# Summing both scan directions on chip, and starting the even layer's output product in the gate stage

## The reference, cut to what matters

```python
def head_group_norm(y, w, b):
    mean = jnp.mean(y, axis=-1, keepdims=True)
    var = jnp.mean(jnp.square(y - mean), axis=-1, keepdims=True)
    yn = (y - mean) * lax.rsqrt(var + RWKV_GN_EPS)
    return yn * w.reshape(RWKV_HEADS, RWKV_HEAD) + b.reshape(RWKV_HEADS, RWKV_HEAD)

def even_output(p, y, bon, conv_w, lnx_w, lnx_b, w_out):
    a_out = short_conv_branch(p[..., :A_COLS], conv_w)
    z_b = p[..., A_COLS + RWKV_SHIFT_COLS:]
    rw = head_group_norm(y, lnx_w, lnx_b) + bon
    b_out = rw.reshape(rw.shape[:2] + (RWKV_WIDTH,)) * jax.nn.silu(z_b.astype(jnp.float32))
    return jnp.concatenate([a_out, b_out.astype(p.dtype)], axis=-1) @ w_out
...
x = x + gate[:, None] * y_lat
```

## Time and profile before

| | us |
|---|---|
| median of 3 runs | 3437.85 (3435.22 to 3439.31) |
| the profiled execution's own time | 3434.52 |
| its span, first to last instruction | 3432.7 |
| TensorE busy | 3095.4 (90% of the span) |
| VectorE busy | 2020.2 (59%) |
| ScalarE busy | 1421.9 (41%) |
| GpSimd busy | 435.1 (13%) |

### The profile page before, as it was taken

How to read it: one execution, slowest core, us unless ns; L and a number is a source line. 1 busy time by engine, 2 the same in 40 slices (tenths; PEclk the granted TensorE clock), 3 DMA queues, 4 the chain that set the end, 5 groups by cost and what they waited for, 6 DMA issues and landing times. The chain is left out here.

```text
span 3432.7 us, 59566 instructions
## 1 busy us (share of the span) xinstructions
PE 3095.4 (90%) x25098; PEld 2564.0 (75%) x25098; DVE 2020.2 (59%) x2919; ACT 1421.9 (41%) x2147; POOL 435.1 (13%) x313
## 2 busy tenths in 40 slices
PE   8999998788874999797999999999667899999999
PEld 5878886777772879665999987777445778888887
DVE  6846345567665423353555534755343588888887
ACT  4434433333333223364444432443454455454443
POOL 0222221111111212200000012211011100000000
PEclk9999999799886999998999999999789999999999
DMA  8432223333314311325112113122111322222853
GB/s 306 131 129 106 97 86 125 76 77 85 78 43 166 127 57 62 125 91 175 54 56 62 39 61 128 50 61 90 62 41 45 115 84 78 90 77 78 301 165 123
DMA packets 216552, 343.65 MB, mean 100 GB/s; under 512 B 74208, under 2 KB 148064, under 8 KB 212832
## 3 DMA queue, kind: packets, MB, share of 16 engines
q1 hardware_dynamic: 192384, 252.43, 22.5%
q0 software_dynamic: 23040, 87.04, 7.4%
q10 hardware_dynamic: 864, 0.38, 0.0%
HBM read 243.72 MB, written 96.08 MB: 99 GB/s over the span
## 5 line engine op out<-in xcount | busy, mean ns | idle before, releaser
L60 PE MATMUL ev_ps<-h_hi,even_ring_hi 128*128 128x512 f32 (+1 forms) x792 | 288.0, 364 | 1.3 <-DVE late_area L806 1.3
L62 PE MATMUL ev_ps<-h_hi,even_ring_lo 128*128 128x512 f32 (+1 forms) x792 | 280.4, 354 | 0.0
L61 PE MATMUL ev_ps<-h_lo,even_ring_hi 128*128 128x512 f32 (+1 forms) x792 | 280.4, 354 | 0.0
L60 PE MATMUL ff_ps<-ff_op,ff_w_hi 128*128 128x512 f32 x672 | 263.6, 392 | 13.6 <-DVE ff_w_lo L3505 10.7
L62 PE MATMUL ff_ps<-ff_op,ff_w_lo 128*128 128x512 f32 x672 | 262.8, 391 | 0.0
L61 PE MATMUL ff_ps<-ff_op,ff_w_hi 128*128 128x512 f32 x672 | 262.7, 391 | 0.0
L60 PEld LDWEIGHTS ev_ps<-h_hi,even_ring_hi 128*128 128x128 f32 x792 | 149.6, 189 | 39.9 <-issue 19.8
L3072 ACT ACTIVATE ma_e<-ma_s,ma_nm 128x1280 f32<-128x1280 f32 x64 | 84.9, 1327 | 214.3 <-DVE ma_nm L3108 214.3
L61 PEld LDWEIGHTS ev_ps<-h_lo,even_ring_hi 128*128 128x128 f32 x792 | 149.7, 189 | 21.7 <-issue 1.7
L62 PEld LDWEIGHTS ev_ps<-h_hi,even_ring_lo 128*128 128x128 f32 x792 | 149.6, 189 | 21.2
L60 PEld LDWEIGHTS ff_ps<-ff_op,ff_w_hi 128*128 128x128 f32 x672 | 127.1, 189 | 41.0 <-DVE ff_w_lo L3505 14.5
(11 more groups left out here) (561 smaller groups left out, 8275.9 us busy)
## 6 DMA issues: line engine op xcount, KB each, us to landing
w_up_raw<-in_w_up SPq DMA_DIRECT2D x48, 512.0 KB, 4.4
w_up_raw<-in_w_down SPq DMA_DIRECT2D x34, 512.0 KB, 5.1
even_ring_raw<-in_ev_w_in POOLq DMA_DIRECT2D x33, 512.0 KB, 3.8
late_area<-in_ada_w SPq DMA_DIRECT2D x32, 512.0 KB, 5.3
ffn_mid<-h POOLq DMA_DIRECT2D x24, 512.0 KB, 2.9
ff_mem<-ffn_mid SPq DMA_DIRECT2D x24, 512.0 KB, 11.1
ar<-late_area SPq DMA_DIRECT2D x8, 1280.0 KB, 5.2
bk<-late_area SPq DMA_DIRECT2D x8, 1280.0 KB, 7.0
```

Of the source, the lines that this page charges most:

```text
L60: nc.tensor.matmul(out, w_hi, x_hi, start=start, stop=False, skip_group_check=resumed)
L61: nc.tensor.matmul(out, w_hi, x_lo, start=False, stop=False, skip_group_check=resumed)
L62: return nc.tensor.matmul(out, w_lo, x_hi, start=False, stop=stop, skip_group_check=resumed)
```

## The change

The y of both directions no longer goes to HBM. In the scan, GpSimd puts each half block into a resident array `ysum` (the tensor `y_even`, now in SBUF): the direction that reaches a token first copies, the other adds. `y` then holds only one half block for each d and e, and ScalarE's copy of the next block waits for GpSimd's sum of the one before. GpSimd also loads the first tile of the `odd_ring`, and makes its low part at the stage's end, where ScalarE makes its high part. The tiles of `ev_w_out` in the ring are laid out anew: a ring tile now holds one half (the convolution's or the scan's 512 input columns) of two output tiles m, so tiles 0 to 3 are the convolution's half and 4 to 7 the scan's.

The gate stage also multiplies the convolution's half. Its 24 units (m, token group) are each 4 steps of three matmuls into one of 5 PSUM banks; the first five units are taken side by side, step by step, as the parts of the convolution arrive. VectorE adds gate times each unit to x, which is loaded once, for all 8 tiles, and stays in SBUF. The mean and the variance share one PSUM area, so they alternate. The convolution's loads move from GpSimd's queue to SP's. The output stage then multiplies only the scan's half, 4 steps instead of 8 for each unit, and adds to the resident x.

```diff
-                def store(n):
-                    for d in range(2):
-                        at = first_token(d, n)
-                        done(sp, "y", d, n)
-                        sp.dma_start(g.yT[d][:, :, at:at + P], y[:, n % 2, d]).then_inc(yst[d, n % 2], 16)
-
                 load(0)
                 load(1)
-                for n in range(NB + 1):
-                    if n >= 1:
-                        store(n - 1)
-                    if n + 2 < NB:
-                        load(n + 2)
-                for d in range(2):
-                    for b in range(2):
-                        sp.wait_ge(yst[d, b], 16 * (NB // 2))
+                for n in range(2, NB):
+                    load(n)
...
+                load_tile(pool, ring, 0)
                 pool.wait_ge(consts, 96)
-                for n in range(NB):
+
+                def sum_outputs(n):
+                    if n + 1 < NB:
+                        for d in range(2):
+                            done(pool, "blocks", d, n + 1)
+                    for e in range(2):
+                        for d in range(2):
+                            at = first_token(d, n) + CH * ORDER[d][e]
+                            done(pool, "y", d, n, e)
+                            if comes_first(d, n):
+                                nc.gpsimd.tensor_copy(ysum[:, :, at:at + CH], y[:, d, e]).then_inc(S["ysum", d], 1)
+                            else:
+                                nc.gpsimd.tensor_tensor(ysum[:, :, at:at + CH], ysum[:, :, at:at + CH], y[:, d, e], ALU.add).then_inc(S["ysum", d], 1)
...
+                        if n >= 2:
+                            done(pool, "ysum", d, n - 2)
...
+                for n in range(NB + 1):
+                    if n < NB:
+                        masked_blocks(n)
+                    if n >= 1:
+                        sum_outputs(n - 1)
+                low_of_tile(nc, pool, ring, 0)
+                load_tile(pool, ring, 1)
...
-                        cp(y[:, n % 2, d, :, half(ORDER[d][e])], bC[d][:, 0:256].rearrange("c (p t) -> c p t", p=4)).then_inc(S["y1", d], 1)
+                        if n:
+                            done(act, "ysum", d, n - 1, e)
+                        cp(y[:, d, e], bC[d][:, 0:256].rearrange("c (p t) -> c p t", p=4)).then_inc(S["y1", d], 1)
...
+                high_of_tile(nc, act, ring, 0)
...
-def phase_even_gate(g, mix, ring):
+def phase_even_gate(g, conv_mix, mix, y, x, gate, ring):
...
+    UNITS = [(m, o, n) for m in range(KD) for o, n in GROUPS]
+    FREE = 5
...
+                def load_conv(p):
+                    if p >= 2:
+                        sp.wait_ge(conv_lo, p - 1)
+                    sp.dma_start(conv[:, p % 2], g.mixT[p]).then_inc(conv_in[p % 2], 16)
+
+                def load_x(m):
+                    sp.dma_start(x[:, m, 0:CTX], g.ins["ctxT"][:, m]).then_inc(x_in[m], 16)
+                    sp.dma_start(x[:, m, CTX:T], g.ins["xT"][:, m]).then_inc(x_in[m], 16)
+
+                load_conv(0)
+                load_conv(1)
+                load_x(0)
+                load_conv(2)
+                load_conv(3)
+                for m in range(1, KD):
+                    load_x(m)
...
+                load_extra(0)
+                load_extra(1)
+                for a in range(1, HALF + 1):
+                    low_of_tile(nc, pool, ring, a)
+                    load_tile(pool, ring, a + 1)
+                    if a + 1 < 4:
+                        load_extra(a + 1)
...
+                def step(u, k, resumed=False):
+                    m, o, n = UNITS[u]
+                    t, r = (m // 2) % 2, HALF * (m % 2) + k
+                    mm = product(nc, ps[:, u % FREE, 0:n], (ring.hi[:, t, r], ring.lo[:, t, r]), (c_hi[:, k, o:o + n], c_lo[:, k, o:o + n]),
+                                 k == 0, k == HALF - 1, resumed)
+                    if k == HALF - 1:
+                        mm.then_inc(done, 1)
+
                 mean_of(0)
-                for p in range(4):
-                    if p < 3:
-                        mean_of(p + 1)
-                    variance_of(p)
+                pe.wait_ge(ring.lo_done, 1)
+                for k in range(HALF):
+                    pe.wait_ge(conv_lo, k + 1)
+                    for u in range(FREE):
+                        step(u, k, resumed=True)
+                    if k == 1:
+                        variance_of(0)
+                for u in range(FREE, len(UNITS)):
+                    if u in (6, 10, 14):
+                        mean_of((u - 2) // 4)
+                    if u in (8, 12, 16):
+                        variance_of((u - 4) // 4)
+                    if u % (2 * NG) == 0:
+                        pe.wait_ge(ring.lo_done, u // (2 * NG) + 1)
+                    pe.wait_ge(added, u - FREE + 1)
+                    for k in range(HALF):
+                        step(u, k)
...
+                def split_tile(a):
+                    if a >= 2:
+                        act.wait_ge(done, 2 * NG * (a - 1))
+                    high_of_tile(nc, act, ring, a)
...
+                split_conv(0)
+                split_conv(1)
+                square(0)
+                split_conv(2)
+                split_conv(3)
+                scale(0)
+                split_tile(1)
+                for p in range(1, 4):
                     square(p)
...
+                    scale(p)
+                    split_y(p - 1)
+                    split_tile(p + 1)
                 split_y(3)
...
+                def add(first, last):
+                    for u in range(first, last):
+                        m, o, n = UNITS[u]
+                        if o == 0:
+                            dve.wait_ge(x_in[m], 32)
+                        dve.wait_ge(done, u + 1)
+                        stt(out=x[:, m, o:o + n], in0=ps[:, u % FREE, 0:n], scalar=gate(1 if o < CTX else 0)[:, m:m + 1], in1=x[:, m, o:o + n],
+                            op0=ALU.mult, op1=ALU.add).then_inc(added, 1)
...
                 centre(0)
-                add(2)
-                split_conv(0)
-                centre(1)
-                add(3)
-                split_conv(1)
-                gate(0)
-                centre(2)
-                split_conv(2)
-                gate(1)
-                centre(3)
-                split_conv(3)
-                split_y(0)
-                gate(2)
-                split_y(1)
-                gate(3)
-                split_y(2)
+                for p in range(4):
+                    split_conv(p)
+                gate_y(0)
+                add(0, 6)
+                for p in range(1, 4):
+                    u = 4 * p + 2
+                    centre(p)
+                    split_y(p - 1)
+                    add(u, u + 3)
+                    gate_y(p)
+                    add(u + 3, u + 4)
+                add(18, 20)
                 split_y(3)
+                add(20, 24)
...
-def phase_even_out(g, mix, xs, ssum, gate, scale, ring, a0):
+def phase_even_out(g, mix, x, xs, ssum, gate, scale, ring):
...
                 for m in range(KD):
                     sp.wait_ge(added, NG * (m + 1))
-                    sp.dma_start(g.x1[m], x[:, m % 2, CTX:T]).then_inc(x_stored[m % 2], 16)
...
+                    if m % 2 == 0:
+                        pe.wait_ge(ring.lo_done, HALF + m // 2 + 1)
...
+                    t = (m // 2) % 2
                     for b, (o, n) in enumerate(GROUPS):
-                        for k in range(KD):
-                            mm = product(nc, ps[:, m % 2, b, 0:n], (ring.hi[:, (a0 + m) % 2, k], ring.lo[:, (a0 + m) % 2, k]), [y[:, k, o:o + n] for y in mix],
-                                         k == 0, k == KD - 1)
+                        for k in range(HALF):
+                            r = HALF * (m % 2) + k
+                            mm = product(nc, ps[:, m % 2, b, 0:n], (ring.hi[:, t, r], ring.lo[:, t, r]), [y[:, k, o:o + n] for y in mix],
+                                         k == 0, k == HALF - 1)
                         mm.then_inc(done, 1)
...
+                pairs = g.ins["ev_w_out"].rearrange("(a m) p (h k) c -> h a p m k c", m=2, h=2)
+                ring = open_ring(g, streams, "odd_ring", [pairs[h, a] for h in range(2) for a in range(KD // 2)] + kvrq)
...
+                    with ExitStack() as sums:
+                        ysum = sums.enter_context(nc.sbuf_tensor("y_even", [P, 4, T], F32, side="right"))
+                        phase_scan(g, ysum, ring)
+                        mix = pair(x, "mix_even", [P, KD // 2, T])
+                        x_even = x.enter_context(nc.sbuf_tensor("x_even", [P, KD, T], F32))
+                        conv_mix = pair(sums, "mix_conv", [P, KD // 2, T])
+                        phase_even_gate(g, conv_mix, mix, ysum, x_even, gate(0), ring)
                     xs = [right(f"xs_{part}", [P, KD, T + 2], F32R) for part in ("hi", "lo")]
                     ssum = right("x_squares", [P, T], F32)
```

(2 more changed lines are left out.)

160 lines of the change are left out of this document (62 added, 98 removed).

## The result

The changed kernel took **3417.25 us** by the median of six runs (3410.79 to 3425.26), the kernel before beside it 3434.82; the ratio is **0.9945 (0.9931 to 0.9958)**, so it is faster by 0.55%. Forecast were 3419 and a range of 3405 to 3429. The profiled execution took 3411.99, with a span of 3410.2. A second set of five runs gave 3413.27 and 0.9947 (0.9930 to 0.9964).

What follows compares the result with a forecast made beforehand. TensorE was taken to bound scan and output stage, a chain through three engines the changed gate stage. Output -56, gate +34.9, scan start +1.5 and scan end +0.8 gave -18.8, so 3437.85 becomes 3419 us; range 3405 to 3429.

Steps and rivals of the forecast that it cites:

- Output stage, -56: Output stage: half of each tile's product gone, 6.89 us a tile, 118.2 becomes 62.2 us; -56 (-55 to -57).
- Gate stage, +34.9: Gate stage: a chain through three engines sets its end, 97.9 against 62.95 us now; +34.9 (+27 to +42).
- step 5: Gate stage's end: unit 22 waits for a queued add 0.5, two units 5.5, last add 0.66, reaching 97.9 us.
- step 3: Gate stage: one add 0.5, unit 5 on TensorE 2.76, then the mean of part 1 2.39, reaching 33.0 us.
- the rival with long rounds: Gate stage: falls of clock in each round and slow hand-overs, gate 106, kernel 3427 us; chance 0.14.
- Half clock in the gate stage: Gate stage: every round falls to 1.2 GHz for its whole length, net +11, kernel 3449 us; chance 0.04.
- Ring splits over the gate: Gate stage: GpSimd's split stretches VectorE's gate, +1.96 us for part 0 and 3.0 for three further splits.
- Sums on GpSimd: Scan: a sum takes about 0.65 us and stays hidden in a gap as long as it takes under 1.4.
- The blocked scan: Scan: GpSimd's 40 sums block VectorE, +26 us, net +7, kernel 3445 us; chance 0.03.
- Scan start, +1.5: Scan start: 0.5 MB of the ring's first tile shares the DMA engines with the first loads; +1.5 (0 to 2.4 us).
- Scan end, +0.8: Scan end: GpSimd's two sums, ring split and load issue done at 56.4, last store before about 55.4; +0.8 (0 to +1.5).
- The scan between, 0: Scan: sums hidden, ScalarE's new wait costs nothing, loads some 3 us earlier gain nothing since they weren't waited for.

Runs made afterwards that it cites:

- the reordered kernel: Against the changed kernel: GpSimd's ring split and load ahead of the scan's last sums, and the gate stage rewritten in another queue order; 3386.32 us, 0.9853.
- the kernel with the load moved: Against the changed kernel: GpSimd issues the load of ring tile 1 in the gate stage instead of at the scan's end; 3408.74 us, 0.9929.
- the summing alone: Against the kernel before: y summed on chip, but both halves still multiplied in the output stage; 3416.6 us, 0.9956.
- one instruction moved: Against the changed kernel: on ScalarE, the high half of the part before stands ahead of Ln and Exp in each round; 3399.3 us, 0.9904.

## Why the prediction was right, and where it wasn't

The sum came out at -18.8 us; the medians of the six runs show -17.6, the two traces -21.1 up to the end of the output stage. That it fits so well is partly luck, since three terms were off and cancel: without the 8.5 that the scan lost between its marks, which no term foresaw, the others make some -12.

- **Output stage, -56:** -57.0. A tile takes 6.9, the next stage follows as read.
- **Gate stage, +34.9:** +39.0 from first instruction to last add, inside the +27 to +42. The chain through the queues held step by step; opening, gate and end are each within 0.6. The opening is so by two errors: part 0 of the convolution was split at 7.6 instead of 9.1, its load having taken 4.3, and part 2, asked for then, took 7.7, where 6.3 was forecast for each. The rounds come within 0.7, but the forecast has an add of 0.66 behind the last gate in them, which the measured ones leave out (and step 5 counts the same add once more, 0.5); to the same place it is 57.5 against 58.9. The term that was mis-sized is the clock, first in step 3, 5.6 us forecast and 7.7 measured. TensorE had stood still for 4.58 us, because unit 5 waited for an add that was queued behind the gate, and so the unit ran at the lower clock:

```profile
1081.95 0.79 PE L60 MATMUL eg_ps<-mix_conv_hi,odd_ring_hi 128*128 128x512 f32 x1 [4.58 <-DVE x_even L1521]
1110.81 3.85 PE L1418 MATMUL eg_stat<-eg_sq,ones_sb 128*128 128x512 f32 x6 [3.49 <-ACT eg_sq L1462]
1081.95:1086.88 4.93, 4.93 (x13) 3.88 (x14) 2.31 (x4) 0.00 (x0) 0.92 (x2) 0.54 0.96 356
```

  4.93 us where I had 2.76, at a granted clock of 0.54. I had charged one fall of the clock, for a variance; two variances paid it (3.85 us for the sum at 1110.81, after 3.49 of idling, and 4.37 at 1130.24, after 5.09, where the one at 1093.20 took 2.31). The three falls cost 5.8 where 2.2 was charged, and this is 3.6 of the 4.1 by which the stage was longer than forecast. Its 102 lies halfway between the 97.9 of the sum and the 106 of the rival with long rounds.
- **Half clock in the gate stage** (the rival on the other side): not so. The three rounds, windows:

```profile
1089.22:1107.88 18.66, 18.10 (x84) 13.77 (x82) 9.93 (x10) 5.98 (x5) 3.49 (x3) 1.00 0.09 28
1107.88:1127.31 19.43, 14.34 (x60) 10.33 (x60) 10.20 (x10) 5.98 (x5) 4.56 (x4) 0.91 0.27 95
1127.31:1148.13 20.82, 17.89 (x77) 13.80 (x78) 11.07 (x10) 6.10 (x5) 3.12 (x2) 0.84 0.08 25
```

  The first round passes wholly at 2.4 GHz, the others at 0.91 and 0.84 in the mean. The Trainium skill, "TensorE: Matmul & The Clock Gate", section "HAM oscillation — how this bites in real kernels", has the fall paid in every round of a loop with waits; here two rounds of three paid it, and neither for its whole length, as their means of 0.91 and 0.84 show.
- **Ring splits over the gate:** forecast +1.96 for part 0 and 3.0 for the rounds. Part 0 paid 1.99 (3.54 against 1.55 at L1503, with GpSimd's subtraction at 1075.85); the rounds together 2.7, by L1500's 1.96, 1.98 and 3.42 against 1.55. The Trainium skill, "SBUF — State Buffer", section "Who interferes with whom", says that a VectorE instruction with two inputs in SBUF contends with a GpSimd instruction that reads SBUF, and that one with at most one SBUF input, outside the two-port modes, does not. The trace agrees on both: L1503 reads two inputs in SBUF and was stretched; in the reordered kernel GpSimd's split at 1093.72 lies over three adds of units, which read one operand from PSUM and took 1.80 us, and in the changed kernel three such adds took 1.80 us at 1100.78, while GpSimd's split ran beside them until L1500 had begun, and 1.79 at 1148.05 without one.
- **Sums on GpSimd:** 0.65 forecast for each; a sum took 0.73, a copy 0.40 (20 of each). They are hidden as argued; the masked copies begin when VectorE delivers, and VectorE is not longer busy. The blocked scan did not come: the VectorE instruction that reads the masked copies took 412 to 1473 ns, 424 in the median (L1160), as before.
- **Scan start, +1.5:** +1.2 (24.30 from SP's first load to ScalarE's first copy, 23.13 before).
- **Scan end, +0.8:** wrong, +4.45. The step that failed is "issues a load (0.3 and 0.57 ...): done at 56.4". I let the stage end when the load was issued. It ended 1.5 us after the load had landed, which cost 4.1 us with the issue, as the kernel with the load moved shows. Nothing in my rows showed a stage that ends on a load from GpSimd. (56.4 against 55.4 is 1.0, not the +0.8 stated.)
- **The scan between, 0:** wrong. "Nothing is gained, they weren't waited for" looked at the loads alone and left the stores' own traffic out. In the two traces the stretch is 8.5 shorter, a part of which can be the spread between executions; in the means of the profiles it is 10, in the times some 6, which is not clear of noise.
- **What the sum hid:** I had set -56 against +34.9 and not asked what the summing alone would do. The waiting for y and the four adds went away with the summing, which shortened the gate stage by 14 us; the product that was moved cost the gate stage 53 for the 57 that it saved.

## What to carry to other kernels

Work that is moved under a stage with idle engines is hidden only as far as the order in the queues lets it: fill an engine's wait with what is ready already (here a high half during the wait for the variance), so that nothing stands between the chain's own instructions. When a change has two halves, price each by itself; here one of them was worth 3.6 us in its two stages, which the time can't tell from nothing, 11 with one instruction moved and 23 once the queues were reordered. And look at what the last instruction ahead of a barrier still has running.

## What the runs showed of the hardware that was not expected

- A load issued from GpSimd as the last thing ahead of the barrier held all engines back for 4.1 us (5.6 against 1.5 from the end of the work ahead of it), although no engine used its data before the next stage; the stage began 1.5 us after it landed, whether it landed 3.8 or 4.9 us after its issue. Whether a load from another queue would do the same was not run.
- One stretch of 420 to 442 us in the scan differs by up to 14 us between executions of the same kernel (428.4 and 442.2), without another instruction in it; with stores that no engine waits for in it, it is some 10 us longer in the mean. More than half of either difference is TensorE's busy time for the same matmuls (344.1 and 352.1 us in these two; 339 without stores and 347 with them in the means). What carries this from the stores to TensorE stays open.
